# One store per block of expert rows, 128 pieces in place of four stores of 32

## The chip, the cores and the metric

The kernel runs on one core of a Trainium2 chip. The metric is the device time of one execution in microseconds (us), lower is better. The core has a matrix engine (PE, with its weight loads PEld), a vector engine (DVE), a scalar engine (ACT), GpSimd (POOL) and a queue engine (SP). Sixteen DMA engines move data between HBM and the on-chip memory; transfers issued by SP, ACT and POOL stand in three queues (q1, q10 and q0 in the profile) and share these sixteen engines.

## The reference

The reference is three layers over 512 tokens of width 1024, each a token mixer followed by a mixture of experts. In each expert layer every token picks two experts out of 16 (first layer) or 32 (second and third), and each expert is a gated network of width 512:

```python
h = silu(x_block @ w_gate[e]) * (x_block @ w_up[e])
y_block = h @ w_down[e]
out[token] += gate * y_block[row of token]
```

The choice depends on the data, so how many tokens an expert gets is known only at run time.

## The kernel before

An expert layer sorts its 1024 pairs of token and expert into blocks of `BLK` = 32 rows, each block of one expert, and runs over them. There are 146 blocks in all in this execution. A loop over pairs of blocks (`AHEAD` = 2) runs on each engine, and semaphores order the engines.

For each block PE multiplies 32 rows by gate and up weights (L1315, two halves), ACT takes Silu of each half (L1379), DVE multiplies and turns it (L1531, L1534), PE multiplies by the down weights (L1326), and DVE copies the result from PSUM into a buffer `y_sb[:, b, :]` (L1547). In the second and third layer PE also gathers the rows of the next block (L1292); in the first one POOL loads them from HBM (L1202).

The 32 rows of 1024 columns lie in `y_sb` as four quarters: partitions 32q to 32q+31 hold columns 256q to 256q+255. ACT stores them to `xybuf` in HBM by `store_quarters`, one transfer for each quarter. There are two `y_sb` buffers. At step g, ACT waits until DVE has copied block g-1 (`s_y`), stores two quarters of that block, waits for the first half of gate and up, does Silu, stores the other two quarters, waits for the second half, and does Silu again. DVE may overwrite a buffer only when its store has landed (`s_stored[b]`): the rows of block g-1 must be in HBM before the copy of block g+1, two blocks after their own copy.

SP streams the weights: 6 MB for each expert in three transfers of 2 MB, each 128 pieces of 16 KB. They go to a ring and to further buffers that hold three experts, so a load waits until the expert three before it is done. What sets the order of the loads is SP's program; what sets the order of the stores is ACT's.

The first stage of the program loads small parameters by ACT's queue. How those ten transfers are shaped is of use below (L355 is in `load`):

```python
load(param_rows[0:8, :], b_in[O_XS:O_XS + 8 * P].rearrange("(c p) -> c p", p=P))
load(param_rows[8:16, :], b_in[O_Q:O_Q + 8 * P].rearrange("(c p) -> c p", p=P))
load(param_rows[16:48, :], a["conv_w"][0].rearrange("k (c p) -> (k c) p", p=P))
load(param_rows[48:56, :], a["conv_b"][0].rearrange("(c p) -> c p", p=P))
load(param_rows[56:60, :], b_in[O_Z:O_Z + 4 * P].rearrange("(c p) -> c p", p=P))
load(brow, b_in[O_V:O_V + T].unsqueeze(0))
load(bgate[0:HEADS, :], b_in[O_DT:O_DT + HEADS].unsqueeze(1))
load(bgate[F_ROW:F_ROW + HEADS, :], b_in[O_F:O_F + HEADS].unsqueeze(1))
load(wsmall[:, :, 0:HEADS], wk[:, :, O_DT:O_DT + HEADS])
load(wsmall[:, :, F_ROW:F_ROW + HEADS], wk[:, :, O_F:O_F + HEADS])
```

The last two have 128 partitions of 8 pieces, and `HEADS` is 8.

Of the kernel before, what the change touches and what calls it, by code (L numbers as in the profile page):

```python
# [24 lines left out]
BLK = 32  # L25
BUF_BLOCKS = 72
SPARE_BLOCK = 69
AHEAD = 2
# [48 lines left out]
def build(nc, a, out, stop=None):  # L77
    ctx = ExitStack()
    with ctx:
# [3 lines left out]
        def signal(name):  # L83
            return Signal(ctx.enter_context(nc.semaphore(name)))
# [11 lines left out]
        xybuf = nc.dram_tensor("xybuf", [BUF_BLOCKS * BLK, D], F32).ap()  # L96
# [979 lines left out]
        def project_and_experts(l, alpha, mT, g_src, b_src, g_src_2, b_src_2, last=False):  # L1076
# [6 lines left out]
            def take(*shape, dt=F32):  # L1083
                v = view(arena, at[0], *shape)
                at[0] += int(np.prod(shape))
                return v.bitcast(dt) if dt != F32 else v
# [18 lines left out]
            y_sb = take(AHEAD, D // 4)  # L1105
# [26 lines left out]
            def at_step(n, count):  # L1132
                return steps[n].sem, base[n] + count
# [6 lines left out]
            s_stored = [signal(f"rows_stored{l}_{b}").sem for b in range(AHEAD)]  # L1140
            s_gu, s_silu, s_hT = (s_gu_1, s_gu_2), (s_silu_1, s_silu_2), (s_hT_1, s_hT_2)
            c0 = moe_at[l]
            quarters = [slice(q * BLK, (q + 1) * BLK) for q in range(4)]
            W = D // 4
# [6 lines left out]
            def value(eng, n, low=1, high=MAXB):  # L1151
                return eng.value_load(table[0:1, n], min_val=low, max_val=high)

            with nc.Block() as block:
                @block.sync
                def _(sp):
                    stream_mixer(sp, first + SLOTS, first + SLOTS + 2)
                    sp.wait_ge(*at_step("logits_done", NT))
                    for kind in range(3):
                        sp.dma_start(third_at[kind], expert_src(l, 2, kind)).then_inc(arrived_x[kind].sem, 16)  # L1160
                    sp.wait_ge(*at_step("placed", TABLED))

                    def load(e, q, kind):
                        if q == 2:
                            sp.dma_start(third_at[kind], expert_src(l, e, kind)).then_inc(arrived_x[kind].sem, 16)
                        else:
                            load_expert_chunk(sp, l, e, kind, c0 + 3 * q + kind)

                    def follow(i, q):

                        end = value(sp, bass.ds(3 * i + q + 1, 1))
                        for kind, used_up in enumerate((s_gu[0], s_gu[1], s_down)):
                            sp.wait_ge(used_up, end)
                            load(3 * i + q + 3, q, kind)

                    with sp.Fori(0, (E - 3) // 3) as i:
                        for q in range(3):
                            follow(i, q)
                    for q in range((E - 3) % 3):
                        follow((E - 3) // 3, q)  # L1180
                    if l < 2:
                        for n in range(mixer_at[l + 1], mixer_at[l + 1] + 3):
                            k = (n - SLOTS - c0) // 3
                            e = 3 * (k // 2) + k % 2
                            sp.wait_ge(s_down, value(sp, slice(e + 1, e + 2)))
                            load_chunk(sp, n)
# [156 lines left out]
                @block.scalar  # L1343
                def _(act):
                    for j in range(NT):
                        act.wait_ge(stat.sem, n0["stat"] + j + 1)
                        act.activation(mean_var[:, j, 2:3], mean_var[:, j, 1:2], ACT.Sqrt, bias=eps_ln).then_inc(sq.sem, 1)
                        for c in range(2):
                            act.wait_ge(*at_step("rows_turned", 2 * j + c + 1))
                            act.activation(xT[:, 4 * c:4 * c + 4, j * P:(j + 1) * P],  # L1350
                                           ps[:, 2 * j + c, :].rearrange("p (k t) -> p k t", k=4), ACT.Copy).then_inc(steps["rows_taken"].sem, 1)
                        act.wait_ge(*at_step("scales", j + 1))
                        act.activation(x_tok[:, j, :], x_tok[:, j, :], ACT.Identity, bias=mean_var[:, j, 1:2],
                                       scale=mean_var[:, j, 3:4]).then_inc(steps["normed"].sem, 1)
                    act.wait_ge(*at_step("maxima_taken", 1))
                    act.activation(expo, expo, ACT.Exp).then_inc(steps["exps"].sem, 1)
                    act.wait_ge(*at_step("maxima_taken", 2))
                    act.activation(ratio, ratio, ACT.Exp).then_inc(steps["exps"].sem, 1)

                    def store_quarters(start, b, two):  # L1360
                        for q in two:
                            act.dma_start(xybuf[bass.ds(start, BLK), q * W:(q + 1) * W], y_sb[quarters[q], b, :])\
                               .then_inc(s_stored[b], 16)

                    act.wait_ge(*at_step("places_ready", 2))
                    for b in range(AHEAD - 1):
                        store_quarters((SPARE_BLOCK + b) * BLK, b, range(4))
                    act.wait_ge(*at_step("placed", TABLED))
                    fours = value(act, slice(E + 2, E + 3), high=MAXB // AHEAD)
                    with act.Fori(0, fours) as p:  # L1370
                        act.preload_act_table(ACT.Silu)  # L1371
                        for b in range(AHEAD):
                            g = AHEAD * p + b
                            freed = (b - 1) % AHEAD
                            act.wait_ge(s_y, g + 1)
                            for half in range(2):
                                store_quarters(g * BLK, freed, (2 * half, 2 * half + 1))
                                act.wait_ge(s_gu[half], g + 1)
                                act.activation(silu_g[:, half, :], ps[:, 2 + half, 0:HALF], ACT.Silu).then_inc(s_silu[half], 1)  # L1379
                    act.wait_ge(s_y, AHEAD * fours + 1)  # L1380
                    store_quarters(AHEAD * fours * BLK, AHEAD - 1, range(4))
                    for b in range(AHEAD):
                        act.wait_ge(s_stored[b], fours * 64 + 64)
                    act.activation(spot, eps_ln, ACT.Copy)

                @block.vector
                def _(dve):
# [125 lines left out]
                    def take_inputs(of=ps[:, 5, 0:W]):  # L1513
                        dve.transpose(xg.rearrange("p k s -> p (k s)"), of).then_inc(s_xg, 1)  # L1514

                    dve.wait_ge(*at_step("placed", TABLED))
                    fours = value(dve, slice(E + 2, E + 3), high=MAXB // AHEAD)
# [8 lines left out]
                    with dve.Fori(0, fours) as p:  # L1526
                        for b in range(AHEAD):
                            g = AHEAD * p + b
                            for half in range(2):
                                dve.wait_ge(s_silu[half], g + 1)  # L1530
                                dve.tensor_tensor(hidden[:, half, :], silu_g[:, half, :], ps[:, 2 + half, HALF:P], ALU.mult)\  # L1531
                                   .then_inc(s_h, 1)
                                dve.wait_ge(s_h, 2 * g + 1 + half)
                                dve.transpose(hT[:, 2 * half:2 * half + 2, :].rearrange("p f s -> p (f s)"), hidden[:, half, :])\  # L1534
                                   .then_inc(s_hT[half], 1)
                            dve.wait_ge(s_gu[1], g + 1)
                            if sent:
                                after_b = (b + 1) % AHEAD
                                dve.wait_ge(s_loaded[after_b], p * 64 + 64)
                                take_inputs(x_in[:, after_b, :])  # L1540
                            else:
                                dve.wait_ge(s_gathered, g + 2)
                                take_inputs()
                                hot(2, 2 * g + 4)
                            dve.wait_ge(s_down, g + 1)
                            dve.wait_ge(s_stored[b], p * 64 + 64)
                            dve.tensor_copy(y_sb[:, b, :], ps[:, 4, 0:W]).then_inc(s_y, 1)  # L1547
            for x in arrived_x:
                x.take(16 * (E // 3))
# [1304 lines left out]
```

## Time and profile before

| what | value |
|---|---|
| median of 3 runs | 2680.26 us (2676.49 to 2680.79) |
| the profiled execution's own time | 2675.48 us |
| its span in the profile | 2673.8 us |
| mean granted TensorE clock | 0.951 |
| PE busy | 2275.1 us (85%) |
| ACT busy | 561.3 us (21%) |
| moved by DMA | 635.86 MB |

The span is the part of the execution that the profile covers, 1.7 us less than the execution's own time. Busy PE is a modelled figure: matmuls overlap, and a busy PE may still be waiting for weights between groups.

### The profile page before, as it was taken

The page shows a single profiled execution, that of the slowest core. Times are in us where ns is not written, and L with a number is a line of the kernel's source. Part 1 is how long each engine was busy: PE and PEld are TensorE (multiplying, and loading weights), DVE is VectorE, ACT ScalarE, POOL GpSimd, SP SyncE. Part 2 cuts the span into 40 slices and gives each one's busy share as a digit, 9 for nine tenths or more (in the row PEclk, how much of TensorE's full clock was granted, in tenths as well). Part 3 has the DMA queues.
Part 4 walks back from the last instruction along what each step waited for, and adds up shares of the span by engine and source line. Part 5 has one row for each costly group of instructions (what it writes and reads, how often), then busy time and mean ns, then how long its engine had stood idle before and what let it go on. Part 6 is the DMA issues. An engine that isn't in the chain of part 4 may idle for free. (4 is left out here: it accounts for less than half of the span.)

```text
span 2673.8 us, 86507 instructions
## 1 busy us (share of the span) xinstructions
PE 2275.1 (85%) x37544; PEld 1611.2 (60%) x37545; DVE 1024.7 (38%) x2635; ACT 561.3 (21%) x1213; POOL 290.2 (11%) x493
## 2 busy tenths in 40 slices
PE   8997988788799888999667789978888988779972
PEld 3445546666588745777545543458887466656751
DVE  1206342222553844333212263046765352223324
ACT  2036211111301721111001131034442111111111
POOL 1001222222100010000000010012333100000001
PEclk9998999999899999999988899989999999999996
DMA  8602169998404008889999942000001289999995
GB/s 341 258 32 95 49 248 368 408 375 321 165 32 160 1 18 323 347 327 428 429 428 428 395 144 102 0 25 3 3 5 65 81 343 427 429 428 428 404 428 218
DMA packets 92529, 635.86 MB, mean 238 GB/s; under 512 B 22869, under 2 KB 43609, under 8 KB 58346
## 3 DMA queue, kind: packets, MB, share of 16 engines
q1 hardware_dynamic: 47984, 584.42, 53.0%
q0 software_dynamic: 13008, 29.41, 3.5%
q10 hardware_dynamic: 31402, 20.06, 2.4%
q8 instruction: 106, 1.74, 0.3%
q14 instruction: 29, 0.24, 0.0%
HBM read 588.69 MB, written 45.12 MB: 237 GB/s over the span
## 5 line engine op out<-in xcount | busy, mean ns | idle before, releaser
L1315 PE MATMUL ps<-ring,arena 128*32 128x128 f32 x13184 | 413.2, 285 | 107.8 <-DMA ring<-in_experts 73.5
L1315 PEld LDWEIGHTS ps<-ring,arena 128*32 128x32 f32 x13184 | 382.2, 115 | 152.7 <-DMA ring<-in_experts 71.9
L1379 ACT ACTIVATE arena<-ps 128x64 f32<-128x64 f32 x292 | 65.5, 224 | 1075.9 <-PE ps L1315 962.0
L1531 DVE TENSOR_TENSOR arena<-arena,ps 128x64 f32<-128x64 f32 x292 | 64.7, 222 | 590.6 <-ACT arena L1379 590.6
L1326 PE MATMUL ps<-ring,arena 128*32 128x256 f32 x3296 | 205.0, 384 | 34.6 <-DVE arena L1534 20.6
L1292 PE MATMUL ps<-x_tok,arena 128*32 128x256 f32 x3456 | 214.9, 388 | 15.8 <-DVE arena L1434 8.2
L1315 PE MATMUL ps<-arena 128*32 128x128 f32 x5504 | 175.1, 287 | 51.3 <-DMA arena<-in_experts 40.0
L1315 PEld LDWEIGHTS ps<-arena 128*32 128x32 f32 x5504 | 161.5, 115 | 70.9 <-DMA arena<-in_experts 45.5
L1265 PE MATMUL ps<-ring,arena 128*128 128x512 f32 x384 | 171.9, 604 | 3.4 <-PEq L2696 1.7
L1326 PEld LDWEIGHTS ps<-ring,arena 128*32 128x32 f32 x3296 | 106.7, 110 | 111.6 <-issue 29.0
L1292 PEld LDWEIGHTS ps<-x_tok,arena 128*32 128x32 f32 x3456 | 119.1, 113 | 74.0 <-issue 24.7
L552 PE MATMUL ps<-xt_mem,ring 128*128 128x512 f32 x320 | 137.9, 593 | 0.0
L1547 DVE COPY arena<-ps 128x256 f32<-128x256 f32 x146 | 62.0, 425 | 178.0 <-DMA xybuf<-arena 91.1
L1265 PEld LDWEIGHTS ps<-ring,arena 128*128 128x128 f32 x384 | 73.0, 194 | 89.8 <-issue 89.5
L2010 PE MATMUL ps<-arena,ring 128*128 128x512 f32 x256 | 110.1, 592 | 0.0
L1202 POOL DMA_DIRECT2D arena<-xbuf x176 | 87.7, 499 | 202.8 <-DVE arena L1514 178.3
L552 PEld LDWEIGHTS ps<-xt_mem,ring 128*128 128x128 f32 x320 | 60.6, 190 | 76.5 <-issue 76.4
L1371 ACT ACT_TABLE_LOAD x73 | 93.7, 1283 | 31.0 <-DVE arena L1505 26.3
L1326 PE MATMUL ps<-xt_mem,arena 128*32 128x256 f32 x1376 | 85.8, 385 | 11.6 <-DVE arena L1534 7.1
L1514 DVE STREAM_TRANSPOSE arena<-ps 128x256 f32<-128x256 f32 x107 | 48.2, 450 | 111.5 <-PE ps L1292 106.9
L2010 PEld LDWEIGHTS ps<-arena,ring 128*128 128x128 f32 x256 | 48.6, 190 | 61.6 <-issue 61.6
L1534 DVE STREAM_TRANSPOSE arena<-arena 128x64 f32<-128x64 f32 x292 | 71.8, 246 | 10.0
(476 smaller groups left out, 3106.8 us busy)
## 6 DMA issues: line engine op xcount, KB each, us to landing
ring<-in_experts SPq DMA_DIRECT2D x165, 2048.0 KB, 21.7
arena<-in_experts SPq DMA_DIRECT2D x50, 2048.0 KB, 24.4
xt_mem<-in_experts SPq DMA_DIRECT2D x25, 2048.0 KB
ring<-in_mixer_chunks SPq DMA_DIRECT2D x24, 2048.0 KB, 13.3
xybuf<-arena ACTq DMA_DIRECT2D x608, 32.0 KB, 6.8
xybuf<-arena SPq DMA_DIRECT2D x1, 9216.0 KB, 51.5
xbuf<-arena SPq DMA_DIRECT2D x1, 9216.0 KB, 31.7
arena<-xbuf POOLq DMA_DIRECT2D x176, 32.0 KB, 6.4
```

The costliest lines, as they stand in the source:

```text
L552: ins = pe.matmul(bank, w[:, k, j * P:(j + 1) * P], xT[:, k, :], start=(k == 0), stop=(k == NK - 1))
L1202: pool.dma_start(x_in[to, b, :], xbuf[bass.ds(start, BLK), q * W:(q + 1) * W]).then_inc(s_loaded[b], 16)
L1265: ins = pe.matmul(ps[:, 2 * j + c, :], mT[:, k, j * P:(j + 1) * P], w[:, k, :], start=(k == 0), stop=(k == NK - 1))
L1292: ins = pe.matmul(ps[to, 5, 0:W], one_hot[:, j, :], x_tok[:, j, q * W:(q + 1) * W], start=(j == 0), stop=(j == NT - 1))
L1315: ins = pe.matmul(ps[at, 2 + half, 0:P], xg[:, k, :], w_gu[half][:, k, q, :], start=(k == 0), stop=(k == NK - 1))
L1326: ins = pe.matmul(ps[at, 4, 0:W], hT[:, f, :], w_d[:, f, q * W:(q + 1) * W], start=(f == 0), stop=(f == NT - 1))
L1371: act.preload_act_table(ACT.Silu)
L1379: act.activation(silu_g[:, half, :], ps[:, 2 + half, 0:HALF], ACT.Silu).then_inc(s_silu[half], 1)
L1531: dve.tensor_tensor(hidden[:, half, :], silu_g[:, half, :], ps[:, 2 + half, HALF:P], ALU.mult)\
L1534: dve.transpose(hT[:, 2 * half:2 * half + 2, :].rearrange("p f s -> p (f s)"), hidden[:, half, :])\
L1547: dve.tensor_copy(y_sb[:, b, :], ps[:, 4, 0:W]).then_inc(s_y, 1)
L2010: ins = pe.matmul(bank, w[:, k, j * P:(j + 1) * P], xm[:, k, :], start=(k == 0), stop=(k == NK - 1))
```

## The change

`store_quarters` becomes `store_rows`: one transfer whose HBM side is walked as quarter, row, column (4 x 32 x 256) and whose on-chip side is all 128 partitions of 256 elements. It is issued at the place of the first two quarters, ahead of the wait for the first half of gate and up. The counts that DVE and ACT wait for follow: one transfer adds 16 to `s_stored[b]` where four added 64. Pieces are 1 KB before and after, and 128 for each block.

```diff
-                    def store_quarters(start, b, two):
-                        for q in two:
-                            act.dma_start(xybuf[bass.ds(start, BLK), q * W:(q + 1) * W], y_sb[quarters[q], b, :])\
-                               .then_inc(s_stored[b], 16)
+                    def store_rows(start, b):
+                        act.dma_start(xybuf[bass.ds(start, BLK), :].rearrange("s (q w) -> q s w", q=4), y_sb[:, b, :])\
+                           .then_inc(s_stored[b], 16)
...
                             act.wait_ge(s_y, g + 1)
+                            store_rows(g * BLK, freed)
                             for half in range(2):
-                                store_quarters(g * BLK, freed, (2 * half, 2 * half + 1))
                                 act.wait_ge(s_gu[half], g + 1)
...
-                        act.wait_ge(s_stored[b], fours * 64 + 64)
+                        act.wait_ge(s_stored[b], fours * 16 + 16)
...
-                            dve.wait_ge(s_stored[b], p * 64 + 64)
+                            dve.wait_ge(s_stored[b], p * 16 + 16)
                             dve.tensor_copy(y_sb[:, b, :], ps[:, 4, 0:W]).then_inc(s_y, 1)
```

ACT's rows of one step of the block loop in the first expert layer, before (the names in brackets are the semaphores that a row waits for):

```order
L1371 ACT_TABLE_LOAD
L1375 ISA
L1362 ISA [waits rows_ready0]
L1362 DMA xybuf<-arena 32x256
L1362 ISA
L1362 DMA xybuf<-arena 32x256
L1379 ACTIVATE arena<-ps 128x64 [waits gate_up_first_half_done0]
L1362 ISA
L1362 DMA xybuf<-arena 32x256
L1362 ISA
L1362 DMA xybuf<-arena 32x256
L1379 ACTIVATE arena<-ps 128x64 [waits gate_up_second_half_done0]
```

And the same step after:

```order
L1370 ACT_TABLE_LOAD
L1374 ISA
L1361 ISA [waits rows_ready0]
L1361 DMA xybuf<-arena 4x32x256
L1378 ACTIVATE arena<-ps 128x64 [waits gate_up_first_half_done0]
L1378 ACTIVATE arena<-ps 128x64 [waits gate_up_second_half_done0]
```

The transfers of the third and fourth quarter no longer stand between the two Silus; nothing stands there now. A transfer that was 32x256 is now 4x32x256.

DVE's rows at the end of the first step of that loop, after the change; `rows_stored0_0` is `s_stored[0]`, and the copy is L1547 before and L1546 after:

```order
L1530 TENSOR_TENSOR arena<-arena,ps 128x64 [waits silu_second_half_ready0]
L1532 REGISTER_ALU
L1533 STREAM_TRANSPOSE arena<-arena 128x64 [waits hidden_ready0]
L1538 ISA [waits gate_up_second_half_done0]
L1513 STREAM_TRANSPOSE arena<-arena 128x256 [waits inputs_loaded_1]
L1545 ISA [waits down_done0]
L1546 COPY arena<-ps 128x256 [waits rows_stored0_0]
```

No work of DVE's is added, removed or moved: the copy still waits for the same store of the same buffer.

## Rows read from the trace of the kernel before

**Rows 1.** The page's head: span, engines, clock, DMA by slice.

```profile
span 2673.8 us, 86507 instructions
...
PE 2275.1 (85%) x37544; PEld 1611.2 (60%) x37545; DVE 1024.7 (38%) x2635; ACT 561.3 (21%) x1213; POOL 290.2 (11%) x493
...
DMA  8602169998404008889999942000001289999995
```

**Rows 2.** Stretches: length, engines, granted clock, DMA share, GB/s.

```profile
1080.00:1120.00 40.00, 39.02 (x1092) 31.52 (x1084) 13.86 (x49) 5.91 (x15) 0.00 (x0) 1.00 0.94 388
1120.00:1160.00 40.00, 38.50 (x1049) 30.52 (x1043) 14.54 (x50) 5.44 (x13) 0.00 (x0) 1.00 0.56 224
1160.00:1200.00 40.00, 39.53 (x1100) 31.94 (x1096) 14.06 (x50) 6.54 (x15) 0.00 (x0) 1.00 0.89 367
1200.00:1520.00 320.00, 241.51 (x5772) 181.78 (x5768) 77.71 (x272) 32.70 (x75) 0.00 (x0) 0.90 1.01 428
2200.00:2480.00 280.00, 233.82 (x5928) 181.05 (x5920) 79.63 (x278) 33.14 (x77) 0.00 (x0) 0.95 1.01 428
420.00:620.00 200.00, 166.06 (x4593) 131.03 (x4596) 47.94 (x170) 30.54 (x70) 57.75 (x116) 0.96 0.99 391
```

**Rows 3.** PE's waits from 1200 to 1520 us: total, times, longest.

```profile
PE ps L1315 <- DMA ring<-in_experts: 46.0, 18, 3.3
PE ps L1315 <- DMA arena<-in_experts: 17.6, 6, 3.3
```

**Rows 4.** DMA queues, 1200 to 1520 us: packets, MB, share of 16 engines.

```profile
q1 hardware_dynamic: 9121, 132.93, 97.1%
```

**Rows 5.** DMA queue and issues, 2200 to 2480 us: KB each, us to landing.

```profile
q10 hardware_dynamic: 5881, 4.02, 4.4%
xybuf<-arena ACTq DMA_DIRECT2D x123, 32.0 KB, 7.1
```

**Rows 6.** DMA queues and ACT's issues, whole execution.

```profile
q10 hardware_dynamic: 31402, 20.06, 2.4%
...
xybuf<-arena ACTq DMA_DIRECT2D x608, 32.0 KB, 6.8
```

**Rows 7.** The copy into y_sb (L1547), 420 to 620 us: what it waited for.

```profile
L1547 DVE COPY arena<-ps x29: 424/425/427, 421.3 to 619.2; 128x256 f32<-128x256 f32 x29
...
  DMA xybuf<-arena: 77.9, 23
```

**Rows 8.** Timeline in the first expert layer: start, us, idle before.

```profile
441.47 0.43 DVE L1547 COPY arena<-ps 128x256 f32<-128x256 f32 x1 [2.69 <-DMA xybuf<-arena]
442.07 0.80 ACTq L1362 DMA_DIRECT2D xybuf<-arena  x2
...
443.06 0.80 ACTq L1362 DMA_DIRECT2D xybuf<-arena  x2
...
449.65 0.42 DVE L1547 COPY arena<-ps 128x256 f32<-128x256 f32 x1 [4.26 <-DMA xybuf<-arena]
```

**Rows 9.** Waits in the whole execution, and L1362's spread of landings.

```profile
DVE arena L1547 <- DMA xybuf<-arena: 91.1, 27, 4.6
ACT small L1384 <- DMA xybuf<-arena: 24.0, 3, 10.1
DMA to landing us min/median/max: 1.5/6.8/11.0
```

**Rows 10.** The copy from PSUM in whole, and ACT's store issues.

```profile
L1547 DVE COPY arena<-ps x146: 424/425/427, 394.8 to 2630.2; 128x256 f32<-128x256 f32 x146
L1362 ACTq DMA_DIRECT2D xybuf<-arena x608: 321/322/1122, 368.9 to 2632.2; - x152
```

**Rows 11.** ACT's timeline at the second expert layer's start.

```profile
1031.18 1.75 ACTq L1362 DMA_DIRECT2D xybuf<-arena  x4
1041.26 0.82 ACTq L1362 DMA_DIRECT2D xybuf<-arena  x2
...
1061.10 0.80 ACTq L1362 DMA_DIRECT2D xybuf<-arena  x2
```

More of the change, by code:

```diff
@@ L1358, in _ @@
                     act.activation(ratio, ratio, ACT.Exp).then_inc(steps["exps"].sem, 1)
-                    def store_quarters(start, b, two):
-                        for q in two:
-                            act.dma_start(xybuf[bass.ds(start, BLK), q * W:(q + 1) * W], y_sb[quarters[q], b, :])\
-                               .then_inc(s_stored[b], 16)
+                    def store_rows(start, b):
+                        act.dma_start(xybuf[bass.ds(start, BLK), :].rearrange("s (q w) -> q s w", q=4), y_sb[:, b, :])\
+                           .then_inc(s_stored[b], 16)
                     act.wait_ge(*at_step("places_ready", 2))
                     for b in range(AHEAD - 1):
-                        store_quarters((SPARE_BLOCK + b) * BLK, b, range(4))
+                        store_rows((SPARE_BLOCK + b) * BLK, b)
                     act.wait_ge(*at_step("placed", TABLED))
@@ L1380, in _ @@
                     act.wait_ge(s_y, AHEAD * fours + 1)
-                    store_quarters(AHEAD * fours * BLK, AHEAD - 1, range(4))
+                    store_rows(AHEAD * fours * BLK, AHEAD - 1)
                     for b in range(AHEAD):
-                        act.wait_ge(s_stored[b], fours * 64 + 64)
+                        act.wait_ge(s_stored[b], fours * 16 + 16)
                     act.activation(spot, eps_ln, ACT.Copy)
```

## The prediction

> **What bounds the kernel now.** I read the page's head first. PE is busy for 85% of the span, but DMA has two long runs of nines and a shorter one [rows 1]; those are the three expert layers, so I looked at stretches inside them. In the layers that begin near 1040 and 2165 us the sixteen DMA engines are busy for a share of 1.01 from 1200 to 1520 and from 2200 to 2480 us, at 428 GB/s, while PE has gaps [rows 2]. In the first of these PE waits 63.6 us for gate and up weights alone [rows 3]. So these stretches are as long as the DMA engines' work. From 1080 to 1200 us it is PE that sets the pace, with shares of 0.94, 0.56 and 0.89 [rows 2].
>
> In the first expert layer, 420 to 620 us, the DMA share is 0.99 [rows 2], and a second limit stands beside it: 23 of 29 copies into `y_sb` wait for the store of that buffer, 77.9 us in all [rows 7]. The timeline shows copies at 441.47 and 449.65 us, 8.2 us apart, both held by a store [rows 8]. In the whole execution such waits are 91.1 us, 27 times [rows 9], so the two later layers have next to none.
>
> **How a store moves.** A weight piece of 16 KB holds an engine for 0.61 us: 132.93 MB are 8113 pieces, and 97.1% of 16 x 320 us over 8113 is 0.613 us [rows 4]. ACT's queue has 4.4% of 16 x 280 us = 197 us of engine time for 123 transfers, which are 30.75 blocks: 6.41 us a block, 0.40 us on each of sixteen engines [rows 5].
>
> How many completion packets a transfer leaves can be counted. ACT's queue has 31402 packets [rows 6]. The 608 stores have 32 pieces each, 19456. The ten parameter loads of the first stage have 8, 8, 32, 8, 4, 1, 8, 8, 1024 and 1024 pieces, by the code shown, 2125. There remain 9821 packets that carry no such piece. If each store leaves 16 of them, that is 9728, and the ten loads have 93. Sixteen for each load would be 160. But 8 + 8 + 16 + 8 + 4 + 1 + 8 + 8 + 16 + 16 is exactly 93: a transfer whose first dimension is 8, 4 or 1 leaves 8, 4 or 1, and so works on that many DMA engines; with 32 or 128 it works on 16.
>
> So a store of one quarter puts 2 pieces and 1 completion on each engine, and a block 12 packets. If weight pieces and store packets take turns one for one on an engine, 12 packets need 12 x (0.61 + 0.05) = 7.9 us beside a steady weight stream. The copies that wait for stores are 8.2 us apart [rows 8]. That agrees, and I take the turns as given.
>
> **The change, part by part.**
>
> *Issues.* ACT issued 608 transfers of 0.322 us [rows 10]; 456 go, 147 us of ACT's queue. It is worth nothing where ACT would wait for PE. ACT is busy for 21% of the span [rows 1]. Where a late copy holds ACT, one pair of issues, 0.8 us, leaves the path to the first Silu and another the path to the second; both lie ahead of a landing that is later still (below). I cost this at 0, with the store or the weights as cover. Without it, the 27 copies that are late today [rows 9] could each free 0.8 us, 22 us.
>
> *Engines.* The new transfer has 4 as the first dimension on the HBM side and 128 partitions on the other. No transfer in the trace has two sides that differ so. The nearest rows are the loads with 8, 4 and 1, which went by the first dimension [rows 6]; if both sides must be cut in equal shares, 4 is all that fits. I take four engines; the other end is sixteen. The Trainium skill, page "DMA: Bandwidth & Descriptors", section "Why a DMA increments its semaphore by 16 and not by 1", states this as a rule: the number of engines is the largest up to 16 that divides the slowest dimension larger than 1 of both sides, and for transfers from ACT they are the lowest-numbered ones. The 93 packets agree with the first half; no row here shows which engines are taken, and the sum by the page would be the one that follows.
>
> *Work on four engines.* A block's 128 pieces now stand on four engines, 32 on each. A piece costs at most 6.41/128 = 0.050 us [rows 5], and at least 0.038 us, at the rate of the weight pieces (132.93 MB in 97.1% of 16 x 320 us is 26.7 KB a us) [rows 4]. So a block costs each of the four 1.23 to 1.60 us, where it had 0.40: 0.83 to 1.20 us more. I take 1.05, near the middle. Every weight transfer is spread over all sixteen engines and lands with its slowest one, and in the expert layers the engines are full. With 146 blocks [rows 10] that is 121 to 175 us, and 153 as taken. Of this, the idle time of DMA from 1080 to 1200 us can hide a part: 0.06, 0.44 and 0.11 of 40 us are 24.4 us [rows 2]. I count half, 12 us; none and all are the ends.
>
> *Landing.* A store is now 32 pieces and 1 completion on one engine: beside a steady weight stream 33 x 0.66 = 21.8 us, against 7.9 us before for the four. Two blocks may pass until its buffer is wanted, and the stores of successive blocks stand in one queue, so the copy L1547 will wait while weights flow. Behind it on DVE stands the next block's product of Silu and up (L1531), behind `s_y` ACT's next store and Silu and PE's down product (L1326). But a wait of PE's stops SP, whose loads run three experts ahead at most. Then the weight queue runs dry and the 33 packets go in 33 x 0.05 = 1.7 us. While either queue has work the four engines lose nothing, so this wait mostly trades places with the wait for weights, and the price is the 153 us above. Not hidden are the starts and ends of the three layers: at the start two stores, of 1031.18 and 1041.26 us, stand ahead of the copy before 1061.10 us [rows 11]. They need up to 2 x 21.8 us from 1031, to 1075, where now the copy of the second block comes at about 1060: up to 15 us late. At the ends ACT already waits 24.0 us in three waits for the last stores [rows 9]. I take 20 us for all six places, with 0 and 60 as ends.
>
> *Sum.* 153 - 12 + 20 = 161 us on the profiled execution's own 2675.5 us is 2836.5. The median of the runs is 4.8 us above that execution, so I forecast **2840 us**. The bounds: 121 - 24 + 0 = 97, so 2777; and 175 + 60 = 235, so 2915.
>
> **Rivals.**
>
> *Sixteen engines after all* (the side that ends faster). The 128 partitions could decide. Then a block is 9 packets on each engine, 9 x 0.66 = 5.9 us, all issued at once, and the copies of the first layer no longer wait: up to 91.1 us [rows 9]. But from 420 to 620 us the engines are full at 0.99 [rows 2], so the weights take over as the bound nearly at once, and I give it 10 us: 2670. It decides if the completions a store leaves are 16. Against it speak the 93 packets. 12%. The same page's section "Rules for kernel authors" advises to coalesce many small transfers into one, since small ones are mostly overhead. The trace has a landing of 1.5 us at best and a median of 6.8 [rows 9], so most of a landing here is the turns with the weights.
>
> *Four engines, but in rotation.* If successive stores took different fours, no engine would have more work, and only the landing of 21.8 us and more would hurt, against two blocks of 8.2 us each in the first layer [rows 8]. A store there is late by up to 5.4 us, and in the other layers often behind a wait for weights; with 0.75 us as a mean for each of the 80 experts it is 60 us, 2740. Nothing speaks for or against it. 8%.
>
> *The waits add up.* If the stall and the weights' wait don't trade places, the four engines run dry once for each expert until the next block issues, at least one landing of 1.5 us [rows 9]: 80 x 1.5 = 120 us on top, 2960. Against it speaks that loads run three experts ahead. 10%.
>
> **How the numbers follow.** The forecast has 70%, the rivals 12, 8 and 10. The range must leave out no more than 2 in 10: I leave out sixteen engines and nearly all of the waits' case, and reach down to the rotation: 2735 to 2915. The likeliest case's own range is 2777 to 2915. A change of 0.2%, 5 us, is about what a measurement of this kernel can tell from none. Faster: most of the rival with sixteen engines, 0.08. Same: the rest of it, 0.04. Slower: 0.88.
>
> **What would show it.** ACT's queue with 152 x (128 + 4) + 2125 + 93 = 22282 packets means four engines; 24106 means sixteen. Landings of the store near 20 us in full stretches, and waits of L1546 for `xybuf` in all three layers where two had none, show the turns. A DMA share well below 1 in the stretches where PE waits for weights (twelve engines idle beside four full ones) shows the imbalance; a share that stays at 1.01 speaks for rotation or sixteen. The prediction is wrong if the first dimension of the HBM side doesn't decide, or if the four engines aren't the same ones each time.

## The result and the profile after

The changed kernel takes 2921.13 us (median of 4 runs, 2918.2 to 2931.14) against 2680.53 us of the kernel before: a ratio of 1.0909, 95% interval 1.0887 to 1.0931. It is 241 us slower. The profiled execution took 2931.14 us, 255.7 us more than the profiled one of before. The forecast was 2840, with 2735 to 2915 as its range: right in sign and in its first step, its growth of 160 us too small by a third, and the measured time lies 6 us outside the range.

The page of the changed kernel, its head, DMA slices and queues:

```profile
span 2929.2 us, 85157 instructions
...
PE 2307.3 (79%) x37544; PEld 1630.8 (56%) x37545; DVE 1013.6 (35%) x2635; ACT 555.0 (19%) x1213; POOL 289.5 (10%) x493
...
DMA  9502298875312038678997732000003798887593
...
q1 hardware_dynamic: 47984, 584.42, 49.2%
...
q10 hardware_dynamic: 22282, 20.02, 2.1%
```

ACT's queue has 22282 packets, to the packet what four engines were to give (before: [rows 6]). Weights are the same bytes. The long runs of nines of before [rows 1] are broken: the DMA engines, full before, now have holes. So the time did not go into more DMA work alone; something else holds the loop for part of the time. The waits of the whole execution say what (waiter, what ended the wait, total us, times, longest):

```profile
ACT arena L1378 <- DVE arena L1546: 766.9, 53, 19.2
DVE arena L1546 <- DMA xybuf<-arena: 653.9, 60, 16.7
```

The copy into `y_sb` now waits 653.9 us for stores where it waited 91.1 [rows 9], and ACT waits behind the copy. The timeline of ACT and DVE in the second layer shows three such blocks:

```profile
1423.56 0.42 DVE L1546 COPY arena<-ps 128x256 f32<-128x256 f32 x1 [15.54 <-DMA xybuf<-arena]
1424.16 0.55 ACTq L1361 DMA_DIRECT2D xybuf<-arena  x1
...
1442.48 0.42 DVE L1546 COPY arena<-ps 128x256 f32<-128x256 f32 x1 [15.40 <-DMA xybuf<-arena]
1443.07 0.55 ACTq L1361 DMA_DIRECT2D xybuf<-arena  x1
1443.67 0.34 ACT L1378 ACTIVATE arena<-ps 128x64 f32<-128x64 f32 x2 [18.58 <-DVE arena L1546]
...
1462.30 0.42 DVE L1546 COPY arena<-ps 128x256 f32<-128x256 f32 x1 [16.32 <-DMA xybuf<-arena]
```

Copies stand 18.9 and 19.8 us apart: 33 packets on an engine at 0.57 to 0.60 us each, near the 21.8 us that the prediction worked out. Before, the held copies of [rows 8] were 8.2 us apart, the longest such distance in that trace; most lie between 7.1 and 7.9, 0.59 to 0.66 us for each of 12 packets. One transfer is issued in 0.55 us, four took 0.8 us for each pair.

A held copy also costs clock. PE's down product right behind the copy of 1307.43 us, after 10 us of idle time, and the next one (start, us):

```profile
1309.54 3.64 PE L1326 MATMUL ps<-ring,arena 128*32 128x256 f32 x32 [10.39 <-DVE arena L1533]
1319.03 1.93 PE L1326 MATMUL ps<-ring,arena 128*32 128x256 f32 x32
```

The granted clock was 0.50 in the first (the lower of its two levels) and 1.00 in the second. In whole the mean granted clock is 0.907 against 0.951, and the same 37544 matmuls keep PE busy for 32 us more. How much of the 32 us is on the path isn't shown.

Stretches of the same layers (length, engines, granted clock, DMA share, GB/s) tell what the weights do meanwhile:

```profile
1500.00:1540.00 40.00, 19.52 (x402) 14.29 (x397) 4.69 (x18) 1.96 (x5) 0.00 (x0) 0.74 1.01 428
1340.00:1380.00 40.00, 27.40 (x608) 20.40 (x608) 9.98 (x37) 4.13 (x10) 0.00 (x0) 0.76 0.69 287
1180.00:1220.00 40.00, 39.51 (x1076) 31.57 (x1072) 15.04 (x53) 6.30 (x14) 0.00 (x0) 1.00 0.45 177
...
1350.00:1360.00 10.00, 2.86 (x76) 1.90 (x64) 0.00 (x0) 0.00 (x0) 0.00 (x0) 0.77 1.01 429
1360.00:1375.00 15.00, 12.79 (x313) 9.95 (x317) 5.52 (x20) 2.29 (x6) 0.00 (x0) 0.81 0.22 83
```

From 1500 to 1540 us, where copies are held, DMA is at 1.01 and 428 GB/s, while PE runs half of the time: weights are fetched ahead. From 1180 to 1220 us PE is at 39.5 of 40 us and DMA at 0.45: the buffers of three experts are full, and PE sets the pace. The last two rows show the change from one to the other. A copy is held until 1360.11 us: up to there PE is busy for 2.9 of 10 us and DMA is full, and right behind it PE is busy for 12.8 of 15 us and DMA for 0.22. In that part of the trace, 1300 to 1480 us, it is SP that waits for PE (total us, times, longest):

```profile
SPq L176 <- PE ps L1315: 61.5, 14, 26.8
```

Each of the two limits holds at a time when the other has slack, so a part of their costs adds. It is a part only: the copy waits 563 us longer than before, and the kernel takes 241 us more.

By layer, from the first to the last copy (first and last start stand in the rows), after and then before:

```profile
L1546 DVE COPY arena<-ps x42: 424/424/427, 394.4 to 733.8; 128x256 f32<-128x256 f32 x42
...
L1546 DVE COPY arena<-ps x52: 424/425/427, 1111.3 to 1672.8; 128x256 f32<-128x256 f32 x52
...
L1546 DVE COPY arena<-ps x52: 424/425/426, 2317.6 to 2885.4; 128x256 f32<-128x256 f32 x52
```

```profile
L1547 DVE COPY arena<-ps x42: 424/425/427, 394.8 to 675.8; 128x256 f32<-128x256 f32 x42
...
L1547 DVE COPY arena<-ps x52: 424/425/427, 1050.1 to 1528.2; 128x256 f32<-128x256 f32 x52
...
L1547 DVE COPY arena<-ps x52: 424/425/427, 2176.2 to 2630.2; 128x256 f32<-128x256 f32 x52
```

That is 339.4, 561.5 and 567.8 us, against 281.0, 478.1 and 454.0: 58, 83 and 114 us more, together the 255.7 between the two profiled executions.

### The profile page after: what moved, and what is told of

Same layout as the page of the kernel before. It is cut to its first block and busy times, and to the rows that moved or that the text cites. A ratio compares the mean times of both kernels' runs of the same rounds, so it can differ in the third digit from the quotient of the medians.

```text
span 2929.2 us, 85157 instructions
## 1 busy us (share of the span) xinstructions
PE 2307.3 (79%) x37544; PEld 1630.8 (56%) x37545; DVE 1013.6 (35%) x2635; ACT 555.0 (19%) x1213; POOL 289.5 (10%) x493
## 3 DMA queue, kind: packets, MB, share of 16 engines
q10 hardware_dynamic: 22282, 20.02, 2.1%
## 5 line engine op out<-in xcount | busy, mean ns | idle before, releaser
L1326 PE MATMUL ps<-ring,arena 128*32 128x256 f32 x3296 | 253.0, 450 | 275.2 <-DVE arena L1533 271.7
L1315 PE MATMUL ps<-ring,arena 128*32 128x128 f32 x13184 | 399.8, 280 | 29.0 <-issue 26.3
L1315 PEld LDWEIGHTS ps<-ring,arena 128*32 128x32 f32 x13184 | 381.8, 114 | 67.2 <-issue 60.6
L1326 PEld LDWEIGHTS ps<-ring,arena 128*32 128x32 f32 x3296 | 125.2, 126 | 373.4 <-issue 325.1
L1546 DVE COPY arena<-ps 128x256 f32<-128x256 f32 x146 | 62.0, 425 | 737.6 <-DMA xybuf<-arena 653.9
L1326 PE MATMUL ps<-xt_mem,arena 128*32 128x256 f32 x1376 | 104.7, 450 | 112.1 <-DVE arena L1533 112.0
L1315 PE MATMUL ps<-arena 128*32 128x128 f32 x5504 | 163.3, 276 | 11.9 <-issue 11.9
L1326 PEld LDWEIGHTS ps<-xt_mem,arena 128*32 128x32 f32 x1376 | 52.7, 126 | 152.0 <-issue 132.3
## 6 DMA issues: line engine op xcount, KB each, us to landing
ring<-in_mixer_chunks SPq DMA_DIRECT2D x24, 2048.0 KB, 12.8
```

The source lines that it names most:

```text
L1315: ins = pe.matmul(ps[at, 2 + half, 0:P], xg[:, k, :], w_gu[half][:, k, q, :], start=(k == 0), stop=(k == NK - 1))
L1326: ins = pe.matmul(ps[at, 4, 0:W], hT[:, f, :], w_d[:, f, q * W:(q + 1) * W], start=(f == 0), stop=(f == NT - 1))
```

## The experiments

Two causes were left to tell apart. **Turns**: a store's 33 packets on an engine alternate with weight pieces, the copy waits, and the time is not given back. **Imbalance**: four engines have more work, whoever waits. Most experiments change the third layer alone, since it is the last to route tokens: the two others must stay as before, and did, at 281 to 287 and 477 to 481 us. ACT's queue shows that the edits did what they say. With its stores of that layer taken away it has 21034 packets; it has 28810 with sixteen engines, 28378 with eight and 28162 with four. For 54 stores these are 144, 136 and 132 packets each: 128 pieces and one completion for each engine.

### How many engines: 16, 8, 4

```diff
+                        if last:
+                            if two[0] == 0:
+                                ways = xybuf[bass.ds(start, BLK), :].rearrange("s (q w) -> (s q) w", q=4).rearrange("(s a) w -> a s w", a=16)
+                                act.dma_start(ways, y_sb[:, b, :]).then_inc(s_stored[b], 64)
+                            return
```

with `a=16`, 8 and 4. The last is the changed kernel's transfer. With 16 and 8 a block's rows land in another order in HBM, so the last layer's output is permuted; bytes and pieces are the same.

> Only the third expert layer changes against the kernel before: one transfer of 128 pieces of 1 KB for each block, its HBM side walked as 16 x 8 x 256, so that sixteen DMA engines share it; rows of a block land in another order there (the last layer's output is permuted, no routing changes). Theory T (turns: a store's packets alternate with 16 KB weight pieces, the number of packets on one engine sets how late the copy is): 9 packets an engine in place of 12, 5.9 us, so no wait for stores; the third layer stays at 454 us from first to last copy, total within 5 us of before. Theory M (merging four transfers into one of 128 pieces costs something by itself): total over 2700 us.

> As the run with sixteen, but the HBM side is walked as 8 x 16 x 256, eight engines: 16 pieces and 1 completion on each, 17 x 0.66 = 11.2 us of turns, and 0.8 us of work a block on each of eight engines where it was 0.4. Theory T: blocks that follow each other at 7 us are held, single ones at 15 us are not; the third layer becomes 10 to 50 us longer. Theory I (imbalance: the busiest engines' added work sets the time): 52 blocks x 0.4 us = 20 us longer. Both are near 2700 to 2725 us in total.

> As the two others, with 4 x 32 x 256: the changed kernel's store in the third layer alone. If the layers are independent, the total is 2680 plus the third layer's growth in the changed kernel, 567.8 - 454.0 = 114 us: 2790 to 2800 us. Theory I alone gives 52 x 1.1 = 57 us, 2737.

Measured: 2678.34 us with sixteen, a ratio of 0.9998 (0.9987 to 1.0009); 2703.88 us with eight, 1.0093 (1.0070 to 1.0115); 2786.65 us with four, 1.0402 (1.0381 to 1.0423). The copy's rows of the third layer, for sixteen, eight and four in this order, one kernel each:

```profile
L1552 DVE COPY arena<-ps x52: 424/425/427, 2183.1 to 2635.2; 128x256 f32<-128x256 f32 x52
```

```profile
L1552 DVE COPY arena<-ps x52: 424/425/426, 2180.5 to 2661.3; 128x256 f32<-128x256 f32 x52
...
  DMA xybuf<-arena: 175.4, 34
```

```profile
L1552 DVE COPY arena<-ps x52: 424/425/426, 2180.7 to 2741.2; 128x256 f32<-128x256 f32 x52
...
  DMA xybuf<-arena: 263.9, 26
```

452.1, 480.8 and 560.5 us, against 454.0 before: 2 us less, 27 and 107 us more. One transfer of 128 pieces costs nothing and gains nothing in this layer, where no copy waited for a store before; what costs is the number of engines that it is spread over. With eight, both theories gave about what was seen. With four, imbalance alone (57 us) was too little.

Held copies with eight engines:

```profile
2376.19 0.42 DVE L1552 COPY arena<-ps 128x256 f32<-128x256 f32 x1 [6.28 <-DMA xybuf<-arena]
2385.94 0.42 DVE L1552 COPY arena<-ps 128x256 f32<-128x256 f32 x1 [6.17 <-DMA xybuf<-arena]
```

They are 9.8 us apart, 0.57 us for each of 17 packets, as with 33 packets on four engines.

### Turns alone: 32 small pieces on each of sixteen engines

```diff
+                                act.dma_start(xybuf[bass.ds(start, BLK), :].rearrange("s (q w) -> (s q) w", q=4), y_sb[:, b, :],
+                                              max_dma_last_dim=256).then_inc(s_stored[b], 64)
```

> Third expert layer only, against the kernel before: one transfer of 128 partitions to one contiguous block in HBM (rows permuted in the last layer's output), cut into pieces of 256 bytes. All sixteen engines take part, and each has 32 pieces and 1 completion, as many packets as in the changed kernel, but a quarter of its bytes. Theory T (turns alone stall the copy): waits for stores appear as in the changed kernel, 15 us and more each, and the third layer grows from 454 us by 50 to 110 us. Theory I (only the busier four engines cost): the layer grows by the added engine time of small pieces, at most 52 x 0.3 = 16 us.

Measured: 2749.13 us, 1.0263 (1.0239 to 1.0286).

```profile
L1552 DVE COPY arena<-ps x52: 424/425/426, 2182.7 to 2706.1; 128x256 f32<-128x256 f32 x52
...
  DMA xybuf<-arena: 207.6, 18
```

The layer takes 523.4 us, 69 more than before, though all engines share the work evenly. So turns cost by themselves. Two held copies of this run, and ACT's queue from 2200 to 2480 us:

```profile
2328.32 0.43 DVE L1552 COPY arena<-ps 128x256 f32<-128x256 f32 x1 [15.46 <-DMA xybuf<-arena]
2346.28 0.42 DVE L1552 COPY arena<-ps 128x256 f32<-128x256 f32 x1 [14.60 <-DMA xybuf<-arena]
...
q10 hardware_dynamic: 14088, 3.50, 5.5%
```

The copies are 18.0 us apart, 0.54 us for each of 33 packets, with a quarter of the bytes on an engine: it is the number of packets that counts. Small pieces add engine time too. By the queue's row a store takes 0.58 us on each engine in place of 0.40 [rows 5], 9 us for 52 blocks, so about 60 us are the turns'.

### One large piece on each of four engines

The stores stay as before. Each step gets one more transfer, HBM to HBM in a buffer that the third layer doesn't use.

```diff
+                    def extra(n):
+                        far, near = (xbuf[at:at + BLK, :].rearrange("(a r) d -> a (r d)", a=4)[:, 0:7168] for at in (0, BLK))
+                        act.wait_ge(s_extra, n)
+                        act.dma_start(near, far).then_inc(s_extra, 16)
...
+                            if last:
+                                extra(g * 16 + 16)
```

> The stores are as before (quarters, sixteen engines, 12 packets). In the third layer ACT issues one more transfer in each step, HBM to HBM in a region that nothing reads: 4 pieces of 28 KB, so one piece and one completion on each of four engines, some 1.1 us of work each and hardly a turn; ACT waits for the last step's one first. Nobody else waits for it. Theory I (the four busier engines cost by their work): 52 x 1.1 = 57 us, less what idle engines hide, so the third layer grows by 35 to 60 us and PE waits for weights. If imbalance costs nothing and only turns do: under 10 us.

> The control: the same bytes in 16 pieces of 7 KB, one on each of sixteen engines, 0.27 us of work each. Theory I: 52 x 0.27 = 14 us, and 10 to 16 us measured. If the extra transfer costs by its existence (HBM traffic, ACT's queue) and not by its spread, both runs grow alike.

Measured: 2730.97 us on four, 1.0188 (1.0171 to 1.0205), and 2695.55 us on sixteen, 1.0061 (1.0044 to 1.0078). The copy's rows, four first:

```profile
L1559 DVE COPY arena<-ps x52: 423/424/426, 2179.8 to 2684.4; 128x256 f32<-128x256 f32 x52
...
  DMA xybuf<-arena: 35.8, 19
```

```profile
L1559 DVE COPY arena<-ps x52: 423/425/426, 2179.1 to 2647.5; 128x256 f32<-128x256 f32 x52
```

504.6 and 468.4 us: 51 and 14 us more than before. The same bytes cost 3.5 times as much on four engines as on sixteen, and both totals are near what the engine time gives (57 and 14). But ACT's wait for the extra transfer also stands in its program, 169 us of waits with four and 88 us with sixteen in this layer, and it makes the agreement with 57 partly luck. ACT in the run with four:

```profile
2501.13 0.22 ACT L1387 ACTIVATE arena<-ps 128x64 f32<-128x64 f32 x1 [7.97 <-DMA xbuf<-xbuf]
...
2519.19 0.22 ACT L1387 ACTIVATE arena<-ps 128x64 f32<-128x64 f32 x1 [7.82 <-DMA xbuf<-xbuf]
```

The 28th copy of the layer comes 278.6 us after the first, against 252.9 before and 258.3 in the control: 26 and 5 us, mostly in stretches where DMA was the bound. From the 31st to the 49th copy it is 156.1 us against 133.4, 23 us more. There PE set the pace before at 7.4 us a block, and now a block takes 8.7 us, with ACT's wait in nearly each. So this pair shows that the spread over four engines costs, and of the 51 us some 26 can be imbalance; most of the rest is the wait that the experiment brought in. A cleaner measure of imbalance comes next.

### Short turns for the whole change: weights in pieces of 4 KB

```diff
-            eng.dma_start(slot(n % SLOTS), expert_src(l, e, kind)).then_inc(arrived[n % SLOTS].sem, 16)
+            eng.dma_start(slot(n % SLOTS), expert_src(l, e, kind), max_dma_last_dim=4096).then_inc(arrived[n % SLOTS].sem, 16)
```

and the same for the third expert's loads, in the kernel before and in the changed one.

> The kernel before with expert weights cut into pieces of 4 KB in place of 16 KB. Theory T: a turn beside weights takes 0.16 + 0.05 us in place of 0.66, so the waits of the copy for stores in the first layer (91.1 us) all but vanish; the weights' rate falls by some 4% (a 4 KB piece takes 0.159 us elsewhere in this trace, 16 KB 0.611), which costs up to 40 us where DMA is the bound: 2670 to 2725 us.

> The changed kernel with expert weights cut into pieces of 4 KB: the store still works on four engines, with 32 pieces on each. Theory T: 33 packets need 33 x 0.21 = 6.9 us of turns beside weights in place of 19 to 22, so the copy's 653.9 us of waits for stores fall under 100 us, and the time falls to what four busier engines cost: at most 2680 + 40 (smaller weight pieces) + 146 x 1.1 = 2880, more likely 2760 to 2840 us. Theory I: the added work of four engines is the cause, the time stays near 2900 us or above, with PE now waiting for weights.

Measured: 2690.46 us for before with 4 KB, 1.0043 (1.0027 to 1.0059), and 2806.64 us for the changed kernel with 4 KB, 1.0493 (1.0462 to 1.0523). Smaller turns take 115 us off the changed kernel's time, although such pieces cost the kernel before 10 us. Between the two kernels 116 us are left of 241, so 124 us of the difference went with the long turns. (The pair was not run together; by the two ratios 121 us are left.) The waits of the changed kernel with 4 KB:

```profile
PE ps L1315 <- DMA ring<-in_experts: 129.4, 44, 4.3
...
DVE arena L1546 <- DMA xybuf<-arena: 96.1, 26, 11.4
```

and of before with 4 KB:

```profile
PE ps L1315 <- DMA ring<-in_experts: 84.6, 34, 3.3
```

Waits for stores fell from 653.9 to 96.1 us, and PE waits for weights again, longer than without the change. That is what imbalance would do: 0.8 us for each of 146 blocks. The layers grew by 29, 32 and 52 us over before with 4 KB. The 96.1 us of store waits that remain all lie in the first layer, so a part of its 29 us may be turns. The third layer, changed kernel first:

```profile
L1546 DVE COPY arena<-ps x52: 424/425/426, 2242.0 to 2761.1; 128x256 f32<-128x256 f32 x52
```

```profile
L1547 DVE COPY arena<-ps x52: 424/425/427, 2180.8 to 2648.1; 128x256 f32<-128x256 f32 x52
```

519.1 against 467.3 us. No copy waits for a store in either, nor does ACT wait for anything that was added, so these 52 us are the best measure of imbalance in this layer. With the 60 us of turns they are 112, and the run with four engines measured 107: nearly a sum, though the one was taken with small weight pieces and the other with small pieces of the store. Why the second layer, with as many blocks, lost only 32 us stays open.

### The same transfer from another queue

```diff
+                    if last:
+                        def store_rows(start, b):
+                            pool.dma_start(xybuf[bass.ds(start, BLK), :].rearrange("s (q w) -> q s w", q=4), y_sb[:, b, :])\
+                                .then_inc(s_stored[b], 64)
...
+                                pool.wait_ge(s_y, g + 1)
+                                store_rows(g * BLK, (b - 1) % AHEAD)
...
                     def store_quarters(start, b, two):
+                        if last:
+                            return
```

> Third expert layer only: the changed kernel's transfer (4 x 32 x 256), issued by GpSimd in place of ACT. In the first layer's loads of 32 pieces GpSimd's queue moves packets of 2 KB, two pieces in one, so a store may leave fewer and larger packets. If the packets hold several pieces and successive stores take other engines, neither turns nor imbalance are left and the third layer stays at 454 us, total 2680. If they hold one piece each: as l3_four, 2787.

Measured: 2685.35 us (median of 7), 1.0020 (1.0006 to 1.0033); the third layer took 459.0 us, with no wait for stores. The copy's row, and DMA of 2250 to 2500 us in that kernel:

```profile
L1565 DVE COPY arena<-ps x52: 424/425/427, 2185.6 to 2644.6; 128x256 f32<-128x256 f32 x52
...
DMA packets 10821, 105.48 MB, mean 422 GB/s; under 512 B 3749, under 2 KB 3749, under 8 KB 4598
...
q0 software_dynamic: 3818, 3.52, 4.2%
```

Between 2 and 8 KB there are 849 packets, and 3.52 MB over 849 is 4.1 KB: four pieces are counted as one packet. On four engines that would be 8 large packets for a store in place of 32. The waits for stores are gone, and with them nearly all of the 107 us. Larger packets alone don't explain that: they leave an engine's bytes as they are, and with the same four engines each time at least 52 x 0.83 = 43 us of imbalance would be left by the prediction's lowest cost, where 5 came. Whether successive stores take other engines can't be seen in the profile; that DMA stays full at 422 GB/s fits it. It is not shown, and neither is what it gave that GpSimd, idle in this layer before, issues the store and ACT does not.

### A faster version

The turns bound the kernel before as well, in its first layer. Weight pieces of 4 KB there, or of 8 KB, in that layer alone:

```diff
+            eng.dma_start(slot(n % SLOTS), expert_src(l, e, kind), max_dma_last_dim=8192 if l == 0 else 16384).then_inc(arrived[n % SLOTS].sem, 16)
```

> The kernel before with weight pieces of 4 KB in the first expert layer alone; output as before. With 4 KB everywhere that layer took 268.4 us from first to last copy in place of 281.1, and the two others 14 us more each. Expected: 12 us faster, 2667 us, a ratio of 0.9955; if the shorter first layer is given back later, 1.000.

> The same with pieces of 8 KB in the first layer: a turn of 0.31 + 0.05 us, 12 packets in 4.3 us, which is still less than the 5 to 7 us between copies. The waits for stores fall from 91 us to under 20, and larger pieces keep more of the weights' rate: 10 to 16 us faster, 2664 to 2670 us.

Measured: 2658.76 us with 4 KB, 0.9923 (0.9909 to 0.9937), and 2656.07 us with 8 KB, 0.9918 (0.9904 to 0.9932), where 2667 and 2664 to 2670 us were expected. The first layer with 8 KB:

```profile
L1547 DVE COPY arena<-ps x42: 424/424/426, 394.2 to 656.4; 128x256 f32<-128x256 f32 x42
...
  DMA xybuf<-arena: 7.7, 2
```

262.2 us in place of 281.0, and 7.7 us of waits in place of 91.1 [rows 9]. The total is 24 us less than before, 8 us more than the best that was expected, and less than both kernels of the study. The interval of the ratio is well clear of 1. The DMA share of 0.99 [rows 2] had said that little could be won in this layer; 19 us could.

## Why the prediction was right or wrong

**Four engines: right.** The packets of ten small loads gave the rule, and the changed kernel's 22282 packets confirm it. That sixteen engines would leave the time nearly as it was (the rival) is what the third layer alone showed, 452.1 against 454.0 us. The cost of the issues at 0 was right too in that layer: with sixteen engines three quarters of them went and nothing changed. The first layer, where the rival saw a gain of 10 us and where late copies hold ACT, was not run with sixteen. That shorter turns alone won 19 us there says that the 10 may have been low.

**Work on four engines: right in mechanism, a little large.** The term was 153 us less 12 for idle engines, 141. With short turns 116 us were left, 0.8 us a block where 1.05 was taken; in the third layer alone they left 52 us for 52 blocks.

**Turns: the length was right, the cost wrong.** 33 packets were put at 21.8 us and are 19 to 20. The step that failed reads "While either queue has work the four engines lose nothing, so this wait mostly trades places with the wait for weights", with 20 us for the layers' starts and ends and nothing for the blocks between. It does mostly trade places: the copy waits 563 us longer, and the difference that long turns make is 124 us. But 124 is not 20, nor the 60 of its upper end. Imbalance came out 25 us under its term, turns 104 us over theirs.

What was left out is what comes behind a held copy. While it is held the weights run ahead (DMA at 1.01) until the three experts' buffers are full; then blocks go at PE's own pace, and all engines have holes (0.22 from 1360 to 1375 us, 0.45 from 1180 to 1220 us). Where PE is nearly the bound itself, as in the second of these, it can't win back what it lost. The run with small pieces on sixteen engines shows both cases in the third layer. Its copies lag behind those of the kernel before by 48 us at the 15th and by 32 us at the 17th, where blocks stood 15 us apart before and PE waited for weights: there lost time comes back. From the 37th to the 45th, where blocks stood 7.2 us apart before, the lag stays at 58 us. At the layer's end about 60 us are left. No run gives the loop more buffers, which would test it directly.

The rival "the waits add up" had this sign and said 120 us on top, close to the 124 that were measured, with 2960 us as its total; that came out too high because the sum under it was (161 us, where imbalance alone was 116). Its size was in part luck: it had the engines run dry for 1.5 us at each of 80 experts, and a hole in the trace is far longer (15 us from 1360 to 1375 us).

**Rotation** is not what ACT's queue does: with it no engine would have more work, and the 52 us that the third layer lost with short turns, with no copy waiting for a store, would have no cause. That is argued from the times; which engines are taken, the profile doesn't tell.

**What would show it.** The packets and the copy's waits in all layers came as written. Landings near 20 us are seen only as the distance of held copies; the profile gives no median landing for this store. A DMA share well below 1 where PE waits for weights did not come. In the changed kernel PE hardly waits for weights at all, and where it does, with 4 KB pieces, the share stays near 1. From 1300 to 1500 us, the changed kernel and then the kernel before, both with such pieces:

```profile
1300.00:1500.00 200.00, 136.22 (x2841) 100.60 (x2836) 38.30 (x134) 15.71 (x37) 0.00 (x0) 0.83 0.99 377
```

```profile
1300.00:1500.00 200.00, 132.97 (x3008) 97.52 (x3001) 40.84 (x142) 17.23 (x39) 0.00 (x0) 0.90 1.03 411
```

The rate fell by 8% and the share by 4%, so the sign was only half there. Why the share stays near 1 with four engines busier than twelve is open.

## What to carry to other kernels

Before transfers are merged, look at the first dimension on both sides: merging four transfers of 32 rows into one of 4 x 32 rows put 128 pieces on four DMA engines in place of sixteen, and the same 128 pieces on sixteen engines cost nothing. Count packets on the busiest engine, not transfers: beside a stream of large pieces each packet waited for about one, so here a small transfer took its packets on an engine times the other stream's piece, and cutting the large stream's pieces in half was worth more than touching the small one. Two limits that hold at different times can cost more than the larger of them: a stall is only free if whoever stalls has slack later. And an experiment that adds a transfer adds the wait for it; look at where in the layer the time grew before a total that fits is believed.

## What the runs showed of the hardware

Beside the stream of 16 KB weight pieces, held copies stood 9.8 us apart with 17 packets of a store on an engine, 18.9 to 19.8 us with 33, and 18.0 us with 33 packets of a quarter of the size: 0.54 to 0.60 us a packet, whatever its bytes. A transfer of the same shape went in packets of 1 KB from ACT's queue and of 4 KB from GpSimd's (849 packets of that size, nearly all of 3.52 MB), and cost 107 us the one way and 5 us the other. Pieces of 4 KB for all weights cost the second and third layer 13 to 15 us each (492.6 and 467.3 us against 478.1 and 454.0), while a store's landing in whole fell from a median of 6.8 to 4.7 us. With these pieces the busy share of the DMA engines was 0.99 at 377 GB/s and 1.03 at 411 GB/s, so a share near 1 doesn't tell a full set of engines from an uneven one.
